# A decoder layer on one core: weights split one stage ahead, a new order of copies and projections in the local attention, and one subtraction per token tile in the merge

## The reference

```
proj = h @ w_in                      # q,k,v of both branches, two gates
qs = q_b.reshape(B, T, KV_HEADS=4, GROUP=4, 64); ks, vs likewise
s = einsum(q, [previous block, own block] of k) * 64**-0.5    # blocks of 128
p = sink_softmax(s, band mask, sink)
o_b = einsum(p, v)
merged = sigmoid(gate_a) * (o_a @ w_br_gdn) + sigmoid(gate_b) * (o_b @ w_br_swa)
return merged @ w_out
```

## Time and profile before

| | us |
|---|---|
| three runs, median | 2680.87 (2676.24 to 2685.32) |
| the profiled execution | 2685.98, its span 2684.3 |
| delta rule of the samples | 918.6 to 1060.9 of the span |
| window attention of the prompt | 1060.9 to 1375.6 |
| window attention of the samples | 1375.6 to 1404.3 |
| merge | 1404.3 to 1806.3 |

### The profile page before, as it was taken

The page is one execution under the profiler, slowest core; times in us unless marked ns, Lnnn a source line. Parts: engine busy times, 40 slices in busy tenths (PEclk is TensorE's granted clock), DMA queues, the critical chain, the costliest instruction groups (busy, mean ns, idle before and its releaser), DMA issues. The chain is left out here.

```text
span 2684.3 us, 35792 instructions
## 1 busy us (share of the span) xinstructions
PE 2282.2 (85%) x13120; PEld 1977.3 (74%) x13121; DVE 1568.4 (58%) x2044; ACT 1143.1 (43%) x1614; POOL 389.8 (15%) x394
## 2 busy tenths in 40 slices
PE   4689889989987698789759999988939999999990
PEld 2378888888886585667538999986837888888870
DVE  2355665565565422255536454535558898889885
ACT  3243243243333300234324333323317778777773
POOL 1011120120221212022211010101011111111103
PEclk8899999999998885899869999998959999999995
DMA  8411121121020214410034545446249999999965
GB/s 322 175 43 48 34 66 34 32 66 49 19 65 22 75 32 117 165 24 1 3 111 132 145 136 144 137 130 191 94 198 343 401 407 403 402 404 406 402 240 220
DMA packets 309859, 432.17 MB, mean 161 GB/s; under 512 B 57698, under 2 KB 250706, under 8 KB 289731
## 3 DMA queue, kind: packets, MB, share of 16 engines
q1 hardware_dynamic: 288764, 369.53, 39.7%
q0 software_dynamic: 11296, 39.46, 3.9%
q10 hardware_dynamic: 9720, 22.11, 2.1%
HBM read 375.98 MB, written 57.10 MB: 161 GB/s over the span
## 5 line engine op out<-in xcount | busy, mean ns | idle before, releaser
L2636 DVE TENSOR_TENSOR ex_w_r<-ex_w,ex_wh 128x2048 fp32r<-128x2048 f32 x198 | 447.0, 2286 | 61.7 <-ACT ex_wh L2578 61.5
L2578 ACT ACTIVATE ex_wh<-ex_w 128x2048 fp32r<-128x2048 f32 x198 | 379.1, 1917 | 120.3 <-PE ex_up L2533 41.4
L2003 DVE TENSOR_TENSOR mg_w_r<-mg_w,mg_wh 128x1024 fp32r<-128x1024 f32 x96 | 135.1, 1413 | 132.7 <-ACT mg_wh L1959 132.7
L1959 ACT ACTIVATE mg_wh<-mg_w 128x1024 fp32r<-128x1024 f32 x96 | 101.6, 1058 | 210.0 <-DVE mg_out L2028 118.9
L894 PE MATMUL gd_ps<-hh,gd_wh 128*128 128x352 f32 x368 | 122.8, 334 | 10.7 <-ACT preS L614 10.7
L1946 PE MATMUL mg_psum<-hh,mg_wh 128*128 128x352 f32 x384 | 124.8, 325 | 7.0 <-DVE mg_w_r L2003 7.0
L1946 PE MATMUL mg_psum<-mg_xl,mg_wh 128*128 128x352 f32 x384 | 125.4, 327 | 0.0
L1946 PE MATMUL mg_psum<-hh,mg_w_r 128*128 128x352 f32 x384 | 124.1, 323 | 0.0
L1946 PE MATMUL mg_psum<-hT_r,mg_wh 128*128 128x352 f32 x384 | 123.8, 322 | 0.0
L894 PE MATMUL gd_ps<-hh,gd_w_r 128*128 128x352 f32 x368 | 118.3, 321 | 0.0
L894 PE MATMUL gd_ps<-hT_r,gd_wh 128*128 128x352 f32 x368 | 118.0, 321 | 0.0
(11 more groups left out here) (618 smaller groups left out, 6119.6 us busy)
## 6 DMA issues: line engine op xcount, KB each, us to landing
ex_w<-in_w_gate_dram SPq DMA_DIRECT2D x66, 1024.0 KB, 8.0
ex_w<-in_w_up_dram SPq DMA_DIRECT2D x66, 1024.0 KB, 7.5
ex_w<-in_w_down_dram SPq DMA_DIRECT2D x66, 1024.0 KB, 8.5
ada_w<-in_w_ada_dram SPq DMA_DIRECT2D x24, 1024.0 KB, 15.8
mg_w<-in_w_in_dram SPq DMA_DIRECT2D x48, 512.0 KB, 3.7
expert_out_scratch<-ex_y ACTq DMA_DIRECT2D x33, 512.0 KB, 7.8
gd_w<-in_w_in_dram SPq DMA_DIRECT2D x32, 512.0 KB, 4.6
mg_w<-in_w_br_gdn_dram SPq DMA_DIRECT2D x24, 512.0 KB, 3.7
```

The source lines that it names most:

```text
L1959: nc.scalar.activation(wh[q][:], wl[q][:], ACT.Copy).then_inc(w_high, 1)
L2003: nc.vector.tensor_tensor(wl_r[q][:], wl[q][:], wh[q][:].bitcast(F32), ALU.subtract).then_inc(w_low, 1)
L2578: nc.scalar.activation(wh[at][:], wl[b][u][:], ACT.Copy).then_inc(w_high, 1)
L2636: nc.vector.tensor_tensor(wl_r[b][u][:], wl[b][u][:], wh[at][:].bitcast(F32), ALU.subtract).then_inc(w_low, 1)
```

## The change

1. The weights of the first key and the first query unit (`wk`, `wq[0]`) are loaded, rounded and subtracted inside the delta stage. ScalarE rounds them after its last `values`; VectorE subtracts them in three parts of 1024 columns behind the updates of pairs 0, 1 and 2. SyncE issues the five loads ahead of two output stores.
2. Six units instead of three come before block 0, and they alternate between two PSUM banks. The other 24 lie one to a block; blocks 0, 21, 25 and 27 to 31 have none. Before, blocks 7, 20, 23 and 26 to 31 had none (block 4 only "rows"), block 0 had three, and 2, 3 and 18 had two.
3. `high_q(1)` and `low_q(1)` move from ahead of block 0 to the end of block 1.
4. VectorE's `ptcopy(n - 2)` moves from the front of block n to its end.
5. The cached keys of the samples are loaded during the prompt's attention, no longer at the start of the samples'. That stage now loads, rounds and subtracts the merge's first two gate weights and the first group of the delta branch.
6. In the merge the rounded copy itself (`mg_xh`) is the high part, and the low part is written over the tokens: one subtraction per tile and group, all on VectorE. GpSimd has no work left there.

```diff
@@ delta_sample, VectorE, end of each pair
+                    if i == 0:
+                        dve.wait_ge(wk_high, 1)
+                        nc.vector.tensor_tensor(c.wk_r[:], c.wk[:], c.wkh[:].bitcast(F32), ALU.subtract)
+                    elif i < 3:
+                        dve.wait_ge(wk_high, 2)
+                        at = slice((i - 1) * KD // 2, i * KD // 2)
+                        nc.vector.tensor_tensor(c.wq_r[:, at, :], c.wq[:, at, :], c.wqh[:, at, :].bitcast(F32), ALU.subtract)
@@ window_prompt
-        first = [("k", 0, 0), ("q", 0, 0, 0), ("q", 0, 1, 0)]
+        first = [(t, 0) + x + (u,) for u in range(2) for t, x in (("k", ()), ("q", (0,)), ("q", (1,)))]
...
+        for body, unit in ((1, ("q", 0, 0, 2)), (2, ("q", 0, 1, 2)), (3, ("k", 0, 2)), (3, ("rows", 0)),
...
+            return pv if place[unit] in (1, 3, 5) else pj
...
-                load_k(0)
-                load_q(0)
                 sp.dma_start(nsink[:], sinks.to_broadcast([P, QH])).then_inc(sk_loaded, 16)
                 load_q(1)
+                sp.dma_start(c.kc[:], cache_k[0].rearrange("b w h d -> w b (h d)")).then_inc(kc_loaded, 16)
...
-                high_k(0)
-                high_q(0)
                 for unit in first:
                     evac(unit)
-                high_q(1)
...
-                    if n in (5, NT + 5):
-                        high_q(2 + n // NT)
+                    if n in (1, 5, NT + 5):
+                        high_q((1, 5, NT + 5).index(n) + 1)
...
                 for n in range(NBLOCKS + 3):
...
-                    if 2 <= n <= NBLOCKS + 1:
-                        ptcopy(n - 2)
                     if n < NBLOCKS:
                         dve.wait_ge(scored, n + 1)
...
                     if n >= 3:
                         outcopy(n - 3)
+                    if 2 <= n <= NBLOCKS + 1:
+                        ptcopy(n - 2)
@@ window_sample
+                for n, at in ((0, CGA), (1, CGB)):
+                    sp.dma_start(c.mw[n][:], kmajor(w_in[0])[:, :, at:at + P]).then_inc(c.mw_loaded[n], 16)
...
+                act.wait_ge(oa_loaded, 16)
+                nc.scalar.activation(c.mx1[:], c.oaT[:, :, 0:C3], ACT.Copy).then_inc(c.mx_round, 1)
@@ merge
-            @block.gpsimd
-            def _(pool):
-                for g in range(G):
-                    pool.wait_ge(x_low, 2 * g + 2)
-                    nc.gpsimd.tensor_tensor(high_of(2, g), x_of(2, g), xl[2][:].bitcast(F32), ALU.subtract).then_inc(x_high_b, 1)
...
-                    nc.vector.tensor_tensor(xl[n][:], x_of(n, g), xl[n][:].bitcast(F32), ALU.subtract).then_inc(x_low, 1)
-                    if n == 1:
-                        dve.wait_ge(x_low, 2 * g + 1)
-                        nc.vector.tensor_tensor(high_of(n, g), x_of(n, g), xl[n][:].bitcast(F32), ALU.subtract).then_inc(x_high, 1)
+                    nc.vector.tensor_tensor(low_of(n, g), x_of(n, g), xh[n][:].bitcast(F32), ALU.subtract).then_inc(x_low, 1)
```

More of the change, by code:

```diff
@@ L1379, in window_prompt @@
         k = Kit(nc, ctx)
[L1380 to L1383, removed]
+        wq1, wq1_r = k.sb_reused("wp_wq1", [P, KD, 2 * P])
+        wq, wq_r = (c.wq, wq1), (c.wq_r, wq1_r)
+        wqh = (c.wqh, k.sb("wp_wqh1", [P, KD, 2 * P], F32R))
+        wk, wk_r, wkh = c.wk, c.wk_r, c.wkh
         qT = k.sb("wp_qT", [P, 2, T])
@@ L1403, in window_prompt @@
         c_merged = c.merged.rearrange("(k p) t -> p k t", p=P)
-        first = [("k", 0, 0), ("q", 0, 0, 0), ("q", 0, 1, 0)]
+        first = [(t, 0) + x + (u,) for u in range(2) for t, x in (("k", ()), ("q", (0,)), ("q", (1,)))]
         plan = {n: [] for n in range(NBLOCKS)}
[L1407 to L1419, removed]
+        for body, unit in ((1, ("q", 0, 0, 2)), (2, ("q", 0, 1, 2)), (3, ("k", 0, 2)), (3, ("rows", 0)),
[4 rows of a table added]
+            plan[body].append(unit)
         order = list(first)
@@ L1423, in window_prompt, with bank_of @@
         place = {unit: n for n, unit in enumerate(order)}
+        assert len(order) == 8 * 3 + 2 * 3 + PAIRS
+        def bank_of(unit):
+            return pv if place[unit] in (1, 3, 5) else pj
         def ready(n):
@@ L1503, in evac @@
                     act.wait_ge(proj, place[unit] + 1)
+                    src = bank_of(unit)
                     if unit[0] == "rows":
@@ L1631, in project @@
                         for v, (a, x) in enumerate(((high, c.hh), (high, c.hT_r), (low, c.hh))):
-                            last = nc.tensor.matmul(pj[:, 0:C3], a(m), x[:, m, at], start=(m == 0 and v == 0), stop=(m == KD - 1 and v == 2))
+                            last = nc.tensor.matmul(bank_of(unit)[:, 0:C3], a(m), x[:, m, at], start=(m == 0 and v == 0), stop=(m == KD - 1 and v == 2))
                     last.then_inc(proj, 1)
@@ L1801, in _ @@
                     nc.scalar.activation(KT[:, 4 * m:4 * m + 4, :].rearrange("p u q -> p (u q)"), B[m][:], ACT.Copy).then_inc(kt_out[1], 1)
+                for n in range(2):
+                    act.wait_ge(c.mw_loaded[n], 16)
+                    nc.scalar.activation(c.mwh[n][:], c.mw[n][:], ACT.Copy).then_inc(c.mw_high, 1)
                 act.wait_ge(vec, 11)
@@ L1840, in _ @@
                 step(nc.vector.tensor_tensor(es[:], nm[:], nsk[:], ALU.subtract))
+                for q in range(2):
+                    dve.wait_ge(c.mw_high, q + 1)
+                    nc.vector.tensor_tensor(c.mw_r[q][:], c.mw[q][:], c.mwh[q][:].bitcast(F32), ALU.subtract).then_inc(c.mw_low, 1)
                 dve.wait_ge(exped, 2)
@@ L1909, in load_next @@
                         load(q, at)
-                for q in range(4):
+                for q in range(2, 4):
                     load(q, 0)
@@ L1982, in body @@
                     act.dma_start(c.merged[bass.ds(j * P, P), g * R:(g + 1) * R], out[b][:]).then_inc(stored[b], 16)
-                for q in range(2):
-                    high(q, 0, 16)
-                rounded(1, 0)
                 rounded(2, 0)
@@ L2030, in body @@
                         split(2, g + 1)
-                low(0, 0)
-                low(1, 0)
-                split(1, 0)
                 split(2, 0)
```

111 lines of the change are left out of this document (68 added, 43 removed), and 4 rows, old and new, of the table plan.

## The result

| | us |
|---|---|
| before, median of 4 runs | 2683.1 (2676.24 to 2686.33) |
| after, median of 4 runs | 2585.78 (2583.63 to 2593.91) |
| ratio, 95% interval | 0.9646 (0.9616 to 0.9676) |
| the profiled execution after | 2583.63, its span 2581.9 |

The kernel after is 97 us faster; 78 were forecast. The forecast of 2603 lies 17 us above the result.

The account below looks back on a forecast made before the run. TensorE (PE) was taken to bound both stages, through its waits and clock. Prompt's attention 54 saved plus merge 24, after 1.2 lost ahead of it, made 78: median 2680.87 to 2603. Range 2586 to 2626; the mechanism's own 2588 to 2620.

Parts of the forecast that it names:

- Start and first weights: Start of the prompt's attention: PE no longer waits for the first weights, 6.5 us saved; delta stage cost 0, upper bound 5.
- rival 4: Delta stage: the moved loads disturb it and it gives back 5 us or some more, 2608 to 2615; chance 0.05.
- Weights of iteration 1, 14.4 + 2.7: Prompt's attention: rounding them after block 1's exponentials removes PE's 14.39 us wait and 2.7 of slow clock, together 17.1 saved.
- Unit waits, 5: Prompt's attention: alternating banks and one unit per block leave about one of some 8 waits of 0.65 us; 5 saved.
- The loop, 29.1: Prompt's attention: VectorE's copy coming last opens a three-engine loop of 6.98 us; blocks without a unit save 29.1 in all.
- Rival 1: Prompt's attention: ScalarE's half of the copy still closes the loop, so the 29.1 us are not saved, 2632; chance 0.08.
- rival 2: Prompt's attention: VectorE and GpSimd hinder each other; five last blocks lose 1.9 us each, 2613; chance 0.06.
- Rival 3: Prompt's attention: PE's clock is granted at the lower level; with half its full-speed need slow, 2711; chance 0.03.
- Weight steps: Prompt's attention: waits on weight rounding and subtraction inside the loop, 9.7 us in all; equal to before, but 1.6 lost to slow products.
- Samples' attention, +1.2: Samples' attention: added weight subtractions and delta token rounding and subtraction lose 1.2 us net, bounds -1 and 3.
- Merge, 24.9: Merge: 6.0 saved at the start, 14.4 of waits at group borders, 4.5 of slow products; 24.9 us in all.
- perhaps 8 more than I count: Prompt's attention: all slow stretches, 41 us of lowered clock, could go, of which perhaps 8 us were not counted.

Follow-up runs that it names:

- two experiments: Part 4 undone in the kernel after: 0.9767 of before, prompt's attention 34.5 us longer; part 4 put alone into the kernel before: 0.9865, that stage 36.7 us shorter.
- the run of part 4 alone: The kernel before with only VectorE's copy of block n-2's transposed weights moved behind block n's reduce and mask: 0.9865 of before, 36 us faster.
- the run with added work: The kernel before plus 20 unread products in each of its nine blocks without a projection unit: 0.9964 of before, some 10 us faster.

## Why the prediction was right, and by how much it missed

- **Start and first weights.** Forecast 6.5; PE's first product came at once, 6.6 saved. Right. The delta stage paid nothing (142.4 and 142.2 us, both at clock 0.68): rival 4 is out.
- **Weights of iteration 1, 14.4 + 2.7.** The wait has gone, but the reason given, the later rounding, is not what it hangs on. Rounding later brings 6.7 us by itself, since 8.9 us of waits come back; in the kernel after it makes no difference. There the load comes early enough, by part 1 as SyncE's rows have it, with part 2's units in front.
- **Unit waits, 5.** One bank for the first six units costs 2.1 us of idle time and, with it, 3 to 5 of busy time. About right in size.
- **The loop, 29.1.** Measured 34.5 and 36.7 by two experiments. The mechanism was right, and so was the tail: 4.04 to 4.44 per block against 4.3. Rival 1 (ScalarE's half of the copy) wanted 6.98, rival 2 (VectorE beside GpSimd) over 6. All 64 masking operations of VectorE's, those beside GpSimd's among them, take 0.68 to 0.69 us in the kernel after; before they took 0.68. Rival 3 (a slower clock) came out the other way round: PE's clock in the stage rose from 0.87 to 0.98, and in the last blocks (1275.3 to 1297.6) it was 1.00, though PE waited there.
- **Weight steps.** Forecast 2.9 for each of three and 1.0 for the keys, 9.7 in all. Measured 3.18, 2.82, 2.81 and 0.93, 9.7. The same steps before were put at 10; they were 3.42, 1.55 and 3.40, 8.4.
- **Samples' attention, +1.2.** The -2.5 of the table is clock: with this stage's code of before the run of part 4 alone took 26.6 us at clock 0.63. Like with like, it is +0.1 to +0.5 at the lower clock (28.8 to 28.9 against 28.4 to 28.7) and -0.5 to +0.1 at the higher (26.2 to 26.7 against 26.6). The forecast of +1.2 was too high.
- **Merge, 24.9.** Measured 25.4 and 24.8. Right, term by term: of 6.0 + 14.4 of waits 20.3 us of idle time went, of 4.5 for the clock 5.1 us of busy time. The start's wait is 1.7 with the barrier, the others 0.3.

The mechanism was right, and the term that was mis-sized is the price of the clock. The forecast said "Behind it 15 us ran at clock 0.82, that is 15 * 0.18 = 2.7", took 1.6 back, and bounded the rest by "perhaps 8 more than I count". PE's busy time fell by 21 to 23 us. Some 9 of these were in the loop's term already: 35.3 us of excess, of which PE waited 26.1 in those nine blocks. With 2.7 less 1.6 that makes 10, and 11 to 13 us were in no term. The idle time fell by 44.8, where the sum held some 44. That is the surplus of the stage, 68.2 or 65.7 against 54, and both lie outside its own bounds of 45 and 62.

The trace of before had it. The loop was read off a block at full clock and taken for all blocks with a unit. But nine of the blocks 5 to 27 last 7.60 to 10.00 us from negation to negation, not 6.98, most of them behind a wait of PE; they come to 11.3 us over (four more, with weights or two units, last 8.79 to 11.78). In the run with added work 7.8 of these 11.3 are gone and 1.0 came back in a block beside them. The sum also left out block 4, which had only the two transposes and in which PE waited 3.43 us for GpSimd; now it has a unit, and this wait has gone. That the result still meets the low end of the range owes something to the range's width: the surplus was larger than the 8 us allowed for the clock.

Not tested by themselves: part 1 and part 5, whose gains are read from the timelines only. Nor is the rest of the surplus divided between blocks.

## What to carry to other kernels

When PE waits in some steps, do not price the wait alone: compare the same operation before and after it, and list the length of all steps, not of one; a step behind a gap may run at half the clock, as the transposes at 1306.69 did. An engine's copy that can be done last in its step should not stand first where the result of a neighbour's chain waits behind it. And a wait that ends late by a load may be gone for another reason than the moved load: undo each part alone before it gets the credit.

## What was not expected of the hardware

- Useless work made the kernel faster: 180 products of 352 columns in gaps, and 0.9964 (0.9943 to 0.9986) of the time; the stage was 6.2 us shorter.
- The delta stage, whose PE work is the same 693 instructions, took 142.0 to 142.4 us at clock 0.68 in eight of fourteen profiles, 138.9 at 0.70 in one, 133.7 to 134.0 at 0.73 in four and 130.8 at 0.75 in one: 11.5 us from the clock alone, since PE's busy time falls by 12.5 (127.4 to 114.9). Of the five kernels without part 1 four had 142 and one 138.9; of the nine profiles with it four had 142. Whether part 1 makes the better clock likelier was not tried. The samples' attention has two lengths in the same code, 26.2 us at clock 0.65 and 28.8 at 0.56. Together the two could cover some 14 of the 21 us by which single executions of one variant spread (2560.8 to 2582.2), though only profiled executions show their stages. So a difference of 5 us in the whole time needs the stage's own length to be seen.
